# One statistics pass for the final and the recurrent norm, the context norm moved into the feed-forward, and an earlier value transpose, in a two-block float32 model

## What is computed

```python
h = first_block(x, c, ctx, ...)      # mixer, feed-forward, mixer, feed-forward
return rmsnorm(h, final_g)           # the end of the first block

# second block: x_lat is that result, x_ctx is a new input, ctx_2
h_lat = rmsnorm(x_lat, norm_pre[0]) * (1 + sc_l) + sh_l
h_ctx = rmsnorm(x_ctx, norm_pre[0]) * (1 + sc_c) + sh_c
y_lat, y_ctx = hgrn2_mixer(h_lat, h_ctx, ...)    # gated recurrence, 16 heads, both directions
x_lat = x_lat + gt_l * rmsnorm(y_lat, norm_post[0])   # then the same with latent attention
```

## Time and profile before

| | |
|---|---|
| median of 3 runs | 3622.75 us (3618.31 to 3626.05) |
| the profiled execution | 3622.84 us |
| its span, first to last instruction | 3621.1 us |
| TensorE matmul busy | 93% |
| VectorE / ScalarE / GpSimd busy | 52% / 33% / 29% |
| mean granted TensorE clock | 0.953 |

### The profile page before, as it was taken

The page is one execution under the profiler, slowest core; times in us unless marked ns, Lnnn a source line. Parts: engine busy times, 40 slices in busy tenths (PEclk is TensorE's granted clock), DMA queues, the critical chain, the costliest instruction groups (busy, mean ns, idle before and its releaser), DMA issues.

```text
span 3621.1 us, 54512 instructions
## 1 busy us (share of the span) xinstructions
PE 3355.2 (93%) x21552; PEld 2785.5 (77%) x21552; DVE 1892.2 (52%) x2914; ACT 1195.5 (33%) x1907; POOL 1044.3 (29%) x476
## 2 busy tenths in 40 slices
PE   6998899999998879999999999999997897999988
PEld 4776788888876657877788888888886786777766
DVE  4455520002346653005648787878787434565656
ACT  3443211111224532112234343434342132555542
POOL 2331534455532035768500000000000451111125
PEclk8999999999999989999889999999998897999999
DMA  6222223233210024544211111111112111111012
GB/s 251 88 76 105 105 93 133 98 133 122 82 64 24 7 85 160 185 177 143 93 54 51 54 48 56 46 52 42 47 42 94 36 61 56 35 41 41 35 58 82
DMA packets 82996, 294.52 MB, mean 81 GB/s; under 512 B 8208, under 2 KB 10256, under 8 KB 81936
## 3 DMA queue, kind: packets, MB, share of 16 engines
q1 hardware_dynamic: 76096, 274.30, 21.5%
q10 hardware_dynamic: 6736, 17.83, 1.3%
HBM read 275.32 MB, written 16.78 MB: 81 GB/s over the span
## 4 chain that ended last, share of the span: by engine, by line
PE 85%; DVE 7%; ACT 3%; DVEq 2%; issue 2%; DMA 1%; ACTq 0%; SPq 0%
PE ps L549 41%; PE ps L635 17%; PE ps L1126 5%; PE ps L1006 2%; PE ps L611 2%; PE ps L1169 2%; PE ps L857 1%; PE ps L1194 1%; PE ps L1077 1%; PE ps L1213 1%; PE ps L1067 1%; PE ps L587 1%; PE ps L959 1%; ACT arena L1528 1%; PE ps L711 1%
## 5 line engine op out<-in xcount | busy, mean ns | idle before, releaser
L481 POOL TENSOR_TENSOR ringB_r<-ringA,consts 128x1024 fp32r<-128x1024 f32 x200 | 397.7, 1989 | 1929.8 <-PE ps L1077 1051.3
L549 PE MATMUL ps<-x_r,ringA_r 128*128 128x512 f32 x2648 | 749.1, 352 | 16.7 <-ACT arena L1659 12.0
L549 PE MATMUL ps<-x_r,ringB_r 128*128 128x512 f32 x2648 | 738.9, 349 | 14.0 <-DVE a_r L1890 14.0
L483 POOL TENSOR_TENSOR ringA_r<-ringA,ringB_r 128x1024 fp32r<-128x1024 f32 x200 | 494.4, 2472 | 28.8 <-issue 0.7
L549 PEld LDWEIGHTS ps<-x_r,ringB_r 128*128 128x128 f32 x2648 | 420.6, 189 | 89.2 <-issue 24.5
L549 PEld LDWEIGHTS ps<-x_r,ringA_r 128*128 128x128 f32 x2648 | 419.2, 189 | 87.9 <-ACT arena L1659 14.1
L549 PE MATMUL ps<-a_r,ringA_r 128*128 128x512 f32 x1504 | 386.7, 338 | 0.0
L635 PE MATMUL ps<-a_r,ringB_r 128*128 128x512 f32 (+1 forms) x1440 | 361.6, 360 | 17.6 <-issue 7.3
L1997 DVE TENSOR_TENSOR arena<-arena,ps 128x768 f32 (+1 forms) x44 | 36.1, 821 | 606.6 <-ACT arena L1412 350.9
L549 PE MATMUL ps<-a_r,ringB_r 128*128 128x512 f32 (+1 forms) x1144 | 344.8, 356 | 0.0
L635 PEld LDWEIGHTS ps<-a_r,ringB_r 128*128 128x128 f32 x1440 | 239.9, 191 | 62.9 <-DVE a_r L1940 14.1
(11 more groups left out here) (323 smaller groups left out, 5588.6 us busy)
## 6 DMA issues: line engine op xcount, KB each, us to landing
ringA<-streamA SPq DMA_DIRECT2D x232, 512.0 KB, 3.3
arena<-streamC SPq DMA_DIRECT2D x136, 512.0 KB, 6.8
ringB<-streamB SPq DMA_DIRECT2D x100, 512.0 KB, 3.3
x_scratch<-x ACTq DMA_DIRECT2D x8, 1024.0 KB, 5.3
x<-x_in SPq DMA_DIRECT2D x2, 3072.0 KB, 11.9
x<-x_scratch SPq DMA_DIRECT2D x3, 2048.0 KB, 8.7
a<-streamC SPq DMA_DIRECT2D x8, 512.0 KB, 12.4
x_scratch<-x ACTq DMA_DIRECT2D x2, 1536.0 KB, 7.1
```

Of the source, the lines that this page charges most:

```text
L481: nc.gpsimd.tensor_tensor(high, ring[:, slot, :], ones[:, 0:1].broadcast_to([P, D]), ALU.mult)
L483: nc.gpsimd.tensor_tensor(ring_r[:, slot, :], ring[:, slot, :], high.bitcast(F32), ALU.subtract) \
L549: mm = nc.tensor.matmul(ps[:, bank + half, 0:tn], wk, src[:, k, t], start=k == 0 and i == 0, stop=k == DC - 1 and i == 2)
```

## The change

Norm 4 becomes the context half of the pre norm (width CTX), norm 5 the latent half, taken together with the final norm: from one pass over the squares it forms two sums, of x^2 and of (g x)^2, in two PSUM columns per token tile, and from them both roots. The normed value of the second norm comes straight from the unnormed `x`; `x` itself is scaled by the final norm later, in hg_out (`final_scale`, with the spread root kept in `kept`). The context's squares, root, scaling and split are made by VectorE and ScalarE in the rounds of ffn_in1, whose loops are written out on three engines. The recurrent layer's first ringB loads wait for one slot of ffn_out1 each, and the high and low parts of its tiles 0 and 1 are made in the product's tail. On TensorE the context columns of tiles 0 and 1 (`part`) are multiplied between the steps of the statistics. The last modulation row is folded in pass 0 of ffn_out1. In a head's step `values_to_tokens` stands before the second half of tile 2, and ScalarE's `values` before `gate`. `low` is renamed `weights_low`, and the norm's inner `low` is `norm_low`.

```diff
...
-                 ("final_g", 0, None, None, LAT),
-                 ("norm_pre", 0, "sc", "sh", T), ("norm_post", 0, None, "gt", T),
+                 ("norm_pre", 0, "sc", "sh", CTX), ("norm_pre", 0, "sc", "sh", LAT),
+                 ("norm_post", 0, None, "gt", T),
...
@@ -444,9 +461,11 @@
             sp.dma_start(x[:, :, 0:LAT], x_dram[:, :, 0:LAT]).then_inc(sem("x_back"), 16)
             stream_A("odd_out")
             stream_ffn(1)
-            sp.wait_ge(readA, readA_after("ffn_out1", 1, 11))
             first = START_B["hg"] // RB
-            for lo, hi, store in ((0, 2, False), (2, 2 + HEADS // 2, True), (2 + HEADS // 2, HEADS, False)):
+            for s in range(RB):
+                sp.wait_ge(readA, readA_after("ffn_out1", 1, 8 + min(s, 3)))
+                load_B(first, s)
+            for lo, hi, store in ((1, 2, False), (2, 2 + HEADS // 2, True), (2 + HEADS // 2, HEADS, False)):
...
+            def context_stats():
+
+                pe.wait_ge(sem("sq_added"), ADDED[4] + 1)
+                for t in range(CTX // P):
+                    at = LAT + t * P
+                    mm = nc.tensor.matmul(ps[:, 3, t:t + 1], rstd[:, at:at + P], ones[:, 0:1], start=t == 0,
+                                          stop=True, skip_group_check=True)
...
+            def context_spread():
...
+                pe.wait_ge(sem("rstd_ready"), root_done(4))
+                for t in range(CTX // P):
+                    mm = nc.tensor.transpose(ps[:, 1, t * P:(t + 1) * P], inv[:, QT + t:QT + t + 1].broadcast_to([P, P]), ident)
...
+            def both_sums():
+
+                pe.wait_ge(sem("sq_added"), ADDED[5] + DC - 3)
+                for i, total in enumerate((final_sq, rstd)):
+                    for t in range(QT):
+                        nc.tensor.matmul(ps[:, 5, 2 * t + i:2 * t + i + 1], total[:, t * P:(t + 1) * P], ones[:, 0:1],
+                                         start=i == 0 and t == 0, stop=False, skip_group_check=True)
...
+            def both_squares(c):
+
+                pe.wait_ge(sem("sq_ready"), SQ_AT[5] + c + 1)
+                for t in range(QT):
+                    mm = nc.tensor.matmul(ps[:, 5, 2 * t:2 * t + 2], sq[:, c % 2, t * P:(t + 1) * P], gsq[:, c, :], start=False,
+                                          stop=c == DC - 1, skip_group_check=True)
+                if c == DC - 1:
+                    mm.then_inc(sem("stat_done"), 1)
...
+            def both_spread():
...
+                pe.wait_ge(sem("rstd_ready"), root_done(5))
+                for t in range(QT):
+                    mm = nc.tensor.transpose(rstd_ps(slice(t * P, (t + 1) * P)), both_inv[:, t:t + 1].broadcast_to([P, P]), ident)
...
+            def final_spread():
+
+                for t in range(QT):
+                    mm = nc.tensor.transpose(ps[:, 5, t * P:(t + 1) * P],
+                                             both_inv[:, QT + t:QT + t + 1].broadcast_to([P, P]), ident)
...
+                        if name == "ffn_out1" and g == 0:
+                            if k == 2:
+                                ada_fold(35, 7, 256)
...
                 name = f"ffn_in{l}"
-                with pe.Fori(0, COUNT[name][0]) as g:
...
+                else:
+                    for g in range(COUNT[name][0]):
+                        turn(g)
+                        if g == 2:
+                            context_stats()
+                        if g == 5:
+                            context_spread()
...
                     if follow:
+                        values_to_tokens(nxt)
                         tile(nxt, 2, 0, second)
-                        values_to_tokens(nxt)
                     pairs(h, 3)
...
+                def part(s, ks, bank, t):
+
+                    w_high, w_low = ringA_r[:, s % RH, :], ringB_r[:, s, :]
+                    for k in ks:
+                        w = slice(k * P, (k + 1) * P)
+                        for i, (wk, src) in enumerate(((w_high[:, w], x_r), (w_high[:, w], a_r), (w_low[:, w], x_r))):
+                            mm = nc.tensor.matmul(ps[:, bank, 0:t.stop - t.start], wk, src[:, k, t], start=k == 0 and i == 0,
+                                                  stop=k == DC - 1 and i == 2)
+                    return mm
+
+                context = slice(LAT, T)
+                both_squares(DC - 2)
+                pe.wait_ge(sem("splitB"), splitB_after("hg", 0, 0))
+                pe.wait_ge(sem("a_ready"), a_before(4) + DC)
+                part(0, range(0, 2), 1, context)
+                both_squares(DC - 1)
+                part(0, range(2, 6), 1, context)
+                both_spread()
+                part(0, range(6, DC), 1, context)
+                pe.wait_ge(sem("splitB"), splitB_after("hg", 0, 1))
+                part(1, range(DC), 3, context)
                 for k in range(DC):
-                    tile(0, 0, 0, [k])
-                    tile(0, 1, 2, [k])
+                    pe.wait_ge(sem("a_ready"), a_before(5) + k + 1)
+                    for s in range(2):
+                        mm = part(s, [k], 2 * s, slice(0, LAT))
+                        if k == DC - 1:
+                            mm.then_inc(readB, 1)
+                    if k == 1:
+                        final_spread()
+                pe.wait_ge(sem("rstd_ready"), KEPT)
                 tile(0, 2, 4)
                 values_to_tokens(0)
                 tile(0, 3, 6)
...
-            pe.wait_ge(sem("ada_copied"), 36)
             out_product("ffn_out1", LAT)
-            pe.wait_ge(sem("product_free"), product_free("ffn_out1", 4, DC - 1))
-            ada_fold(35, 4, 0)
-            norm_stats(4)
-            norm_stats(5)
...
+                if n == 5 and c == 0:
+                    nc.scalar.activation(final_sq, src, ACT.Square, scale=SM("final_g")[:, 0:1])
                 nc.scalar.activation(dst, src, ACT.Square).then_inc(sem("sq_ready"), 1)
...
-                r = inv[:, 0:NORMS[n][4] // P]
-                nc.scalar.activation(r, r, ACT.Sqrt).then_inc(sem("rstd_ready"), 1)
+                r = inv[:, QT:NT] if n == 4 else both_inv if n == 5 else inv[:, 0:NORMS[n][4] // P]
+                nc.scalar.activation(r, r, ACT.Sqrt, scale=float(D) if n == 5 else 1.0).then_inc(sem("rstd_ready"), 1)
...
                     for c in range(DC):
...
+                        shifted(n, c)
+                        if n == 5 and c == 3:
+                            act.wait_ge(sem("rstd_spread"), KEPT)
+                            nc.scalar.activation(kept, ps[:, 5, :], ACT.Copy).then_inc(sem("rstd_ready"), 1)
+                        if n == 5 and c == 5:
+                            hg_high(2)
+
+            def hg_high(s):
+
+                act.wait_ge(readA, readA_after("ffn_out1", 1, 8 + s))
+                act.wait_ge(landedB[s], landedB_at("hg", 0))
+                nc.scalar.activation(ringA_r[:, s, :], ringB[:, s, :], ACT.Copy).then_inc(sem("hg_high"), 1)
...
+                else:
+                    for g in range(COUNT[name][0]):
+                        turn(g)
+                        if g == 3:
+                            norm_root(4)
+                        if g == 6:
+                            for c in range(DC):
+                                shifted(4, c)
...
+                    if n == 5 and c in (5, 6):
+                        hg_high(c - 5)
...
                         high(nxt, 4)
+                        values(nxt, 1 - e)
                         gate(nxt, 1 - e, 0, 0)
-                        values(nxt, 1 - e)
                         bounded(G, 1 - e, 0)
...
+            def norm_low(n, c):
...
+            def context_squares():
+
+                t = slice(LAT, T)
+                nc.vector.memset(gsq[:], 1.0)
+                dve.drain()
+                TT(gsq[:, :, 0], SM("final_g"), SM("final_g"), ALU.mult)
+                dve.wait_ge(sem("ctx2_in"), 16)
+                TT(rstd[:, t], x[:, 0, t], x[:, 0, t], ALU.mult)
+                for c in range(1, DC):
+                    TT(sq[:, 0, t], x[:, c, t], x[:, c, t], ALU.mult)
+                    dve.drain()
+                    last = TT(rstd[:, t], rstd[:, t], sq[:, 0, t], ALU.add)
+                    dve.drain()
+                last.then_inc(sem("sq_added"), 1)
...
+            def context_inverse():
+
+                dve.wait_ge(sem("stat_done"), STATS_AT[4])
+                TS(inv[:, QT:NT], ps[:, 3, 0:CTX // P], 1.0 / D, EPS, ALU.mult, ALU.add)
+                dve.drain()
+                nc.vector.reciprocal(inv[:, QT:NT], inv[:, QT:NT]).then_inc(sem("inv_ready"), 1)
...
+            def context_scaled():
...
+                t = slice(LAT, T)
+                dve.wait_ge(sem("rstd_spread"), root_done(4))
+                dve.drain()
+                for c in range(DC):
+                    STT(a[:, c, t], x[:, c, t], coef[:, c, 1:2], ps[:, 1, 0:CTX], ALU.mult, ALU.mult).then_inc(sem("scaled"), 1)
...
+                if n == 5:
```

(51 more changed lines are left out.)

142 lines of the change are left out of this document (83 added, 59 removed).

## The result

| | median | lowest to highest | runs |
|---|---|---|---|
| before | 3622.7 us | 3618.3 to 3626.1 | 6 |
| after | 3607.3 us | 3601.4 to 3611.9 | 6 |

The ratio is 0.9952, 95% interval [0.9942, 0.9962]: 13.8 to 21.0 us faster. Forecast were 3592.1 us, 3580 to 3602 as the range, and a ratio of 0.9915. The same kernel, timed again, gave 3605.9 us beside 3624.6, ratio 0.9949 [0.9936, 0.9962]. The time is outside the range, on its slow side.

What follows compares the result with a forecast made beforehand. TensorE, busy 93% of the span, was taken as the bound. Terms -34.5 + 4.0 + 1.0 + 0.35 - 1.5 = -30.7 us took 3622.8 to 3592.1 us, range 3580 to 3602.

Steps and rivals of the forecast that it cites:

- part 1: From ffn_out1's last matmul to tile 2: one pass for both norms, context columns made earlier; 56.0 becomes 21.5, gain 34.5 us.
- the last 30 context and all latent matmuls with final_spread: End of the new stretch before tile 2: 3.60 for context, 10.90 for 48 latent matmuls, 0.65 for final_spread.
- the 2.4 to the first latent chunk: New stretch: the first latent chunk is ready some 2.4 us after the spread, covered by 30 context matmuls.
- Part 2: Second pass of ffn_out1: three added VectorE STTs queue behind GpSimd and delay out_low; cost 4.0 us, bounds 0 and 9.4.
- Part 4: final_scale in hg_out: eight STTs fit in VectorE's idle 6.6 us between pairs of out_low; cost 0.
- Part 5: Heads: values turned amid the gate tile; the 0.8 us wait goes, select is next; 1.5 us gained over 15 heads.
- Residual and first squares: New stretch: residual of chunk 7 and its square, over both_squares(6) and 6 context matmuls; 1.60 us.
- both_squares(7): New stretch: statistics matmuls of the last chunk, 4 x 0.205 and a start; 0.90 us.
- twelve context matmuls: New stretch: they lie over the inverse and root, 0.12 apart; 1.44 us on the path.
- Rival C: Port costs full turns and TensorE starts the new stretch at its lower clock: 5.4 + 1.8 more, 3599.3; chance 0.16.
- Part 3: ffn_in1: context statistics and transposes put into its rounds; cost 1.0 us, and ada_fold(35) moved to the product, 0.35.
- removing the loop gives nothing: ffn_in1: writing out the loop gains nothing, since rounds start 24.35 us apart, which their matmuls fill.

Runs made afterwards that it cites:

- no_stt: The changed kernel without the added STT in add_square for chunks 1, 2 and 3, against the kernel before: 3597.9 us, ratio 0.9925.
- again: The changed kernel once more, unedited, against the kernel before: 3605.9 us, ratio 0.9949.
- no_ctx: The changed kernel with 36 of the 48 context matmuls left out of the new stretch, against the kernel before: 3600.9 us, ratio 0.9930.
- shift6: The changed kernel with six one-column VectorE memsets ahead of the heads' loop, against the kernel before: 3602.3 us, ratio 0.9945.
- shift12: The changed kernel with twelve one-column VectorE memsets ahead of the heads' loop, against the kernel before: 3602.9 us, ratio 0.9939.
- loops: The kernel before with only ffn_in1's eleven rounds written out on TensorE, ScalarE and VectorE, against the kernel before: 3626.6 us, ratio 1.0012.

## Why the prediction missed

**Right.** The mechanism of part 1 and its cover: TensorE never waits between the product's end and tile 2. Its full-clock terms: both_sums 1.68 (1.70), the last 30 context and all latent matmuls with final_spread 14.97 (15.15), the 2.4 to the first latent chunk 2.5. Part 2 with its place: STTs of 2.2 to 2.7, out_low(30) at 1753.8 (1752.6), 4.0 by no_stt. Part 4: final_scale costs nothing. Part 5: select is next, as the table of waits shows.

**Wrong, by steps.**
- The terms of part 1 between the product and the spread were taken at full clock. Residual and first squares took 2.69 (1.60), both_squares(7) 1.50 (0.90), twelve context matmuls 2.77 (1.44): 3.0, less 0.3 elsewhere, 2.7 in all. Rival C named that fall of the clock, for 1.8, but tied it to full port turns; it came without them.
- Part 5 was forecast as -1.5 for the heads and they took 1.6 more. Its own share lies between -1.0 and +0.8; the step that failed is one that the prediction put at nothing without a reason: that the other 14 parts of a head keep their time if nothing in them is edited. Without part 5 the heads of the changed kernel take 901.4 in place of 898.6, and the written-out rounds alone give 900.1. VectorE's added pauses, 1.0 us more than before, are a part of it at most; where the rest comes from is open.
- "The rest of the kernel is unchanged", which the sum took without saying it, cost 2.8 at norms 6 and 7; 2.0 of it by a meeting with GpSimd and by the clock.
- Part 3 had 1.0 and "removing the loop gives nothing". After's profile gives 0.7, which looks like a hit and is luck: the mean of the thirteen profiles is 2.4, and the rounds no longer keep their 24.35 us.
- 0.7 us between tile 2 and the first head was not followed up.
- The forecast was made against one profile and its own time. Between the gain of 21.4 in the profiles and 15.4 in the medians lie 6 us. Again's profile, which is 15.4 shorter than before's, has 5.6 of them in two places: 3.9 ahead of norm 3 and 1.7 in ffn_in1. The second belongs to part 3. For the first, the thirteen profiles of changed kernels have the transposes of norm 3 at 1381.5 to 1389.1, with 1384.1 in the middle, and the four with the kernel before or small edits of it at 1379.6 to 1385.5. Whether that is scatter alone or the changed program is later there from the start is open. Either way a range that leaves out so much was too narrow.

## To carry to other kernels

When a long idle stretch is taken out, price what is left at the clock that the chip grants in such a place, both ways, and add an allowance for every later norm or short-matmul stretch, since its phase against the clock and against GpSimd moves. Cut several profiles at the same events before calling a small term a hit: one profile gave 0.7 where thirteen gave 2.4. While GpSimd splits weights, give VectorE no further instruction that reads SBUF, with one tensor or two; let TensorE sum squares in a free bank, which cost 0.79 a chunk here and removed a 4.8 us wait. Where two engines share a loop with under 0.2 us of slack, allow a tenth of a per cent for code that only moved.

## What was unexpected of the hardware

- TensorE was at 1.2 GHz for some 6.5 us while it was busy without a gap (6.90 of 6.90, clock 0.51 in after). The same fall came in seven of the nine profiles with a wait of 5 us ahead of it (in after it ended 46 us earlier), one of them with gaps (no_ctx, 5.26 of 6.90).
- A tensor_scalar with one SBUF tensor took 1.93 to 2.44 beside GpSimd, as long as a tensor_tensor; a memset of the same size took 0.48.
- VectorE's pauses without a releaser, 0.15 to 0.56 each, stand at the same instructions in both profiles of the changed kernel (after, again) and moved in shift6 and shift12, where memsets were added ahead.
- Eleven rounds written out in place of a loop made TensorE's rounds some 0.1 to 0.2 us longer each (221.2 in place of 219.2 for nine, in loops), although its work was the same.
